# S5 windows loaded as one DMA a tile and masked on ScalarE, and z's three mixtures formed inside the LoRA products

## What is computed

```python
proj = n1 @ w_in                               # u | r | k | v | z, 512 columns each
# S5 group, on u: 32 groups of 16 channels, 64 complex states per group
x_t = a * x_(t-1) + bbar @ u_t                 # a scan over the tokens
y = c_re @ x_re - c_im @ x_im + d * u
z = gelu(y); out = z * sigmoid(z @ glu_w + glu_b)
# RWKV-7 group, on p = [r|k|v|z]
delta = shifted - p                            # the row before, minus this row
r = r_p + r_d * mu[0]; k = k_p + k_d * mu[1]; v = v_p + v_d * mu[2]
zw = z_p + z_d * mu[3]; za = z_p + z_d * mu[4]; zg = z_p + z_d * mu[5]
decay = exp(-DECAY_SCALE * sigmoid(w0 + tanh(zw @ w1) @ w2))
a = sigmoid(a0 + (za @ a1) @ a2)
g = sigmoid(zg @ g1) @ g2
```

## Time and profile before

| | us |
|---|---|
| median of 3 runs | 1459.41 (1457.45 to 1460.13) |
| the profiled execution | 1459.49 |
| its span | 1457.7 |
| TensorE busy | 1369.6 |
| VectorE busy | 444.9 |
| ScalarE busy | 253.7 |
| GpSimd busy | 55.4 |

### The profile page before, as it was taken

How to read it: one execution, slowest core, us unless ns; L and a number is a source line. 1 busy time by engine, 2 the same in 40 slices (tenths; PEclk the granted TensorE clock), 3 DMA queues, 4 the chain that set the end, 5 groups by cost and what they waited for, 6 DMA issues and landing times.

```text
span 1457.7 us, 21163 instructions
## 1 busy us (share of the span) xinstructions
PE 1369.6 (94%) x8649; PEld 695.7 (48%) x8649; DVE 444.9 (31%) x881; ACT 253.7 (17%) x480; POOL 55.4 (4%) x111
## 2 busy tenths in 40 slices
PE   8958999999999999999999999998998999988997
PEld 5735688866665633434334343343343433433442
DVE  5699846434121321312112111121121111311112
ACT  3223431212223212101101011011010110110102
POOL 4233000000000000000000000000000000000000
PEclk9978999999999999999999999999999999999999
DMA  8960121013939769999999999999999999999994
GB/s 325 203 116 30 62 91 60 32 60 120 388 135 410 279 252 397 401 423 428 427 428 428 428 428 428 428 428 428 428 428 428 428 428 428 428 429 425 428 426 179
DMA packets 43335, 471.84 MB, mean 324 GB/s; under 512 B 4992, under 2 KB 10368, under 8 KB 11520
## 3 DMA queue, kind: packets, MB, share of 16 engines
q1 hardware_dynamic: 37264, 461.42, 76.4%
q10 hardware_dynamic: 6000, 9.41, 3.3%
HBM read 465.33 MB, written 5.48 MB: 323 GB/s over the span
## 4 chain that ended last, share of the span: by engine, by line
PE 71%; DMA 20%; DVE 7%; issue 1%; ACT 1%; ACTq 0%; SPq 0%; DVEq 0%
DMA big<-in_w_gu 18%; PE bank L1189 16%; PE bank L1238 14%; PE bank L716 10%; PE bank L1112 5%; PE bank L979 2%; PE bank L799 2%; PE bank L1302 2%; PE bank L1258 2%; DMA big<-u_windows 2%; PE bank L898 1%; PE bank L1119 1%; PE bank L1214 1%; PE bank L1287 1%; DVE big L1847 1%
## 5 line engine op out<-in xcount | busy, mean ns | idle before, releaser
L1189 PE MATMUL bank<-big 128*64 128x512 f32 x1920 | 427.9, 603 | 27.6 <-DMA big<-in_w_gu 27.4
L1189 PEld LDWEIGHTS bank<-big 128*64 128x64 f32 x1920 | 147.1, 138 | 305.3 <-issue 295.0
L1238 PE MATMUL bank<-big 128*64 128x512 f32 x960 | 209.4, 594 | 0.0
L716 PE MATMUL bank<-big 128*128 128x320 f32 (+1 forms) x688 | 187.5, 430 | 9.1 <-DVE big L1922 6.8
L716 PEld LDWEIGHTS bank<-big 128*128 128x128 f32 x688 | 130.1, 191 | 63.0 <-issue 13.4
L2242 DVE TENSOR_TENSOR big<-big,bank 128x320 f32<-128x320 f32 x120 | 58.6, 488 | 303.0 <-PE bank L1258 297.8
L2228 DVE TENSOR_SCALAR big<-bank 128x512 f32<-128x512 f32 x32 | 22.2, 693 | 391.5 <-PE bank L1189 361.3
L1238 PEld LDWEIGHTS bank<-big 128*64 128x64 f32 x960 | 70.2, 137 | 127.9 <-issue 126.0
L1593 ACT ACTIVATE big<-big 128x512 f32<-128x512 f32 x30 | 18.8, 626 | 448.4 <-DVE big L2228 448.4
L1353 ACT ACTIVATE big<-bank 128x320 f32<-128x320 f32 (+3 forms) x122 | 53.1, 436 | 232.7 <-PE bank L716 41.9
L1112 PE MATMUL bank<-big 128*128 128x512 f32 x192 | 87.1, 603 | 1.4 <-DVE big L2176 1.4
(11 more groups left out here) (408 smaller groups left out, 1146.5 us busy)
## 6 DMA issues: line engine op xcount, KB each, us to landing
big<-in_w_gu SPq DMA_DIRECT2D x128, 2048.0 KB, 25.1
big<-in_w_down SPq DMA_DIRECT2D x62, 2048.0 KB, 22.3
big<-in_dense SPq DMA_DIRECT2D x47, 1024.0 KB, 8.4
big<-u_windows ACTq DMA_DIRECT2D x32, 160.0 KB, 10.4
big<-in_w_down SPq DMA_DIRECT2D x4, 1024.0 KB, 20.8
big<-in_smw SPq DMA_DIRECT2D x1, 1408.0 KB, 19.3
big<-in_xT SPq DMA_DIRECT2D x2, 640.0 KB, 4.6
big<-in_consts SPq DMA_DIRECT2D x1, 1028.5 KB, 14.5
```

What stands on the lines that cost most here:

```text
L716: last = mm(b[:, 0:n], w[:, k, :], src[:, k, :], start=(k == 0), stop=(k == kt - 1))
L1189: last = mm(ps[n][part, :], xte[:, 2 * j + k, part], w[s][:, k, n * 512:n * 512 + 512], start=False, stop=end)
L1238: last = mm(ps[bank][part, :], actT[:, 4 * d + i, part], w[s][:, i, h * 512:h * 512 + 512], start=(d == 0 and i == 0), stop=end)
```

## The change

- `u_windows` gets rows of 320 without zeros between them, channel by channel, the eight groups of a channel behind one another. Each tile of uT is stored by a DMA of its own (`store_rows`), as soon as its rows are there; seven zeros stand ahead of the first. The second u tile is scaled ahead of n1.
- A tile of windows is one DMA of 128 pieces of 10,240 B. What stands in the first columns of a row is then the end of the row before, which the mask takes away. Load 0 is issued between the memory squares and the last two stores, load 1 behind `memsum`, loads 2 and 3 from the list.
- All four masks are ScalarE's, seven activations each, and stand earlier in the list: `win` 0 ahead of k1, `win` 1 ahead of `c` 0.
- z's three mixtures are gone. (z + delta * mu) @ w is formed as z @ w + delta @ (mu * w): `delta` of z is kept in `z_apart`, ScalarE scales the twelve tiles of w1, a1 and g1 by mu (`weigh`), and `lora_up` has twenty-four matmuls.
- The order of the list is new from its third entry on.

```diff
--- before.py
+++ after.py
-MIX_ORDER = [("in", "k0"), ("memsum", 0), ("load", 0), ("in", "k1"), ("f", 0), ("in", "k2"), ("load", 1), ("c", 0), ("in", "k3"),
-             ("par", 0), ("memtotal", 0), ("in", "z0"), ("f", 1), ("in", "z1"), ("win", 0), ("win", 1), ("blk", 0), ("memroot", 0), ("load", 2), ("scan", 0),
-             ("y", 0), ("in", "z2"), ("mix", "k"), ("par", 1), ("in", "z3"), ("out", 0), ("c", 1), ("blk", 1), ("load", 3),
-             ("gelu", 0), ("scan", 1), ("gated", 0), ("y", 1), ("in", "r0"), ("win", 2), ("delta", "z"), ("in", "r1"), ("shares", 0),
-             ("shares", 1), ("out", 1), ("par", 2), ("c", 2), ("in", "r2"), ("blk", 2), ("scan", 2), ("y", 2), ("win", 3), ("gelu", 1), ("gated", 1),
-             ("shares", 2), ("in", "r3"), ("in", "v0"), ("mix", "r"), ("out", 2), ("par", 3), ("in", "v1"), ("c", 3), ("gelu", 2), ("gated", 2),
-             ("blk", 3), ("scan", 3), ("y", 3), ("lora_up", 0), ("in", "v2"), ("in", "v3"), ("kk", 0), ("memnorm", 0), ("out", 3),
-             ("gelu", 3), ("mix", "v"), ("gated", 3), ("lora_down", 0), ("knorm", 0), ("decays", 0), ("memk", 0), ("decay_exp", 0),
-             ("memk", 1), ("memk", 2), ("memk", 3), ("memk", 4), ("memk", 5), ("glu", 0)]
+MIX_ORDER = [("in", "k0"), ("memsum", 0), ("win", 0), ("in", "k1"), ("f", 0), ("in", "k2"), ("win", 1), ("c", 0), ("in", "k3"),
+             ("par", 0), ("memtotal", 0), ("in", "z0"), ("f", 1), ("blk", 0), ("load", 2), ("memroot", 0), ("par", 1), ("scan", 0), ("y", 0),
+             ("in", "z1"), ("mix", "k"), ("blk", 1), ("load", 3), ("out", 0), ("scan", 1), ("y", 1), ("win", 2), ("in", "z2"), ("c", 1),
+             ("win", 3), ("in", "z3"), ("out", 1), ("weigh", 0), ("par", 2), ("gelu", 0), ("gated", 0), ("c", 2), ("in", "r0"), ("delta", "z"),
+             ("blk", 2), ("scan", 2), ("y", 2), ("gelu", 1), ("in", "r1"), ("gated", 1), ("out", 2), ("par", 3), ("in", "r2"),
+             ("gelu", 2), ("c", 3), ("gated", 2), ("blk", 3), ("scan", 3), ("y", 3), ("in", "r3"), ("in", "v0"),
+             ("out", 3), ("mix", "r"), ("lora_up", 0), ("in", "v1"), ("memnorm", 0), ("in", "v2"), ("in", "v3"), ("kk", 0), ("gelu", 3),
+             ("mix", "v"), ("gated", 3), ("lora_down", 0), ("knorm", 0), ("decays", 0), ("memk", 0), ("decay_exp", 0), ("memk", 1),
+             ("memk", 2), ("memk", 3), ("memk", 4), ("memk", 5), ("glu", 0)]
...
-        u_dram = nc.dram_tensor("u_windows", [W5, T + 7], F32)
+        u_dram = nc.dram_tensor("u_windows", [W5 + 1, T], F32)
...
         def S(name):
...
+        z_apart, mu_w1, mu_a1, mu_g1 = R[4], view(RW[5], CT, 64), view(RW[5] + 256, CT, 64), view(RW[5] + 512, CT, P)
...
             def s5_block(ct):
...
-                if ct < 2:
-                    pe.wait_ge(S("uwin"), ct + 1)
-                else:
-                    pe.wait_ge(S("uwin_places"), (BL - 1) * (ct - 1))
+                pe.wait_ge(S("uwin"), (BL - 1) * (ct + 1))
...
             def lora_up():
...
-                pe.wait_ge(S("z_mixed"), 12)
-                for job, w, n, src in (("lw", smw("w1", CT, 64), 64, R[4]), ("la", smw("a1", CT, 64), 64, R[5]),
-                                       ("lg", smw("g1", CT, P), P, R[6])):
+                pe.wait_ge(S("z_apart"), 1)
+                pe.wait_ge(S("weighed"), 3 * CT)
+                for job, w, by, n in (("lw", smw("w1", CT, 64), mu_w1, 64), ("la", smw("a1", CT, 64), mu_a1, 64), ("lg", smw("g1", CT, P), mu_g1, P)):
...
-                        last = mm(b[0:n, 0:T], w[:, k, :], src[:, k, :], start=(k == 0), stop=(k == CT - 1))
+                        mm(b[0:n, 0:T], w[:, k, :], prj["z"][:, k, :], start=(k == 0), stop=False)
+                        last = mm(b[0:n, 0:T], by[:, k, :], z_apart[:, k, :], start=False, stop=(k == CT - 1))
...
             def lora_down():
...
+            def store_rows(ct):
+
+                stored(act, f"u{ct}")
+                to = bass.AP(u_dram, T + ct * P * T, [[T, 8], [8 * T, GC], [1, T]])
+                act.dma_start(to, uT[:, ct, 7:]).then_inc(S(f"u_stored{ct}"), 16)
+
+            def load_windows(ct):
+
+                if ct >= 2:
+                    computed(act, f"loc{ct - 2}")
+                act.wait_ge(S(f"u_stored{ct}"), 16)
+                act.wait_ge(S(f"u_stored{ct - 1}" if ct else "front_stored"), 16)
+                src = bass.AP(u_dram, T + ct * P * T - 7, [[1, BL], [8 * T, GC], [1, 8 * T]])
+                act.dma_start(uwins[ct % 2].rearrange("p g t -> p (g t)"), src).then_inc(S(f"uwin_in{ct % 2}"), 16)
+
+            act.wait_ge(S("u_pad"), 1)
+            act.dma_start(bass.AP(u_dram, T - 7, [[7, 1], [1, 7]]), uT[0:1, 0, 0:7]).then_inc(S("front_stored"), 16)
+            store_rows(0)
+            store_rows(1)
...
-            stored(act, "u3")
-            act.wait_ge(S("u_pad"), 1)
-            act.dma_start(u_dram.ap().rearrange("(c p) t -> p c t", p=P), uT).then_inc(S("u_stored"), 16)
+            load_windows(0)
+            store_rows(2)
+            store_rows(3)
...
             def s5_params(ct):
...
-            def load_windows(ct):
-
-                if ct >= 2:
-                    computed(act, f"loc{ct - 2}")
-                for tap in range(BL):
-                    src = bass.AP(u_dram, ct * P * (T + 7) + tap, [[T + 7, GC], [GC * (T + 7), 8], [1, T]])
-                    act.dma_start(uwins[ct % 2][tap * GC:(tap + 1) * GC], src).then_inc(S(f"uwin_in{ct % 2}"), 16)
-
             def mask_windows(ct):
...
-                act.wait_ge(S(f"uwin_in{ct % 2}"), 16 * BL * (ct // 2 + 1))
+                act.wait_ge(S(f"uwin_in{ct % 2}"), 16 * (ct // 2 + 1))
...
-                    step(af(w[:, j::BL], w[:, j::BL], ACT.Identity, scale=con("window")[:, j:j + 1]), "uwin_places")
-
-            act.wait_ge(S("u_stored"), 16)
+                    step(af(w[:, j::BL], w[:, j::BL], ACT.Identity, scale=con("window")[:, j:j + 1]), "uwin")
+
...
             for kind, n in MIX_ORDER:
...
                 elif kind == "load":
...
-                elif kind == "win" and n >= 2:
+                elif kind == "win":
...
                 elif kind == "memsum":
...
+                    load_windows(1)
                 elif kind == "memroot":
...
+                elif kind == "weigh":
+                    act.wait_ge(S("smw_in"), 16)
+                    for m, (w, by) in enumerate(((smw("w1", CT, 64), mu_w1), (smw("a1", CT, 64), mu_a1), (smw("g1", CT, P), mu_g1))):
+                        for k in range(CT):
+                            step(af(by[:, k, :], w[:, k, :], ACT.Identity, scale=vec("rwkv_mu", 4 * (3 + m) + k)), "weighed")
                 elif kind == "blk":
...
+            u_rows(1)
...
-            u_rows(1)
...
-            def delta(c):
+            def delta(c, d):
...
-                ps_, ds_ = (x[:, :, TP:T].rearrange("p i (s t) -> p i s t", s=NB) for x in (p, DELTA))
-                step(tt(DELTA[:, :, 1:TP], p[:, :, 0:TP - 1], p[:, :, 1:TP], sub))
-                step(ts(DELTA[:, :, 0:1], p[:, :, 0:1], -1.0, None, mul))
+                ps_, ds_ = (x[:, :, TP:T].rearrange("p i (s t) -> p i s t", s=NB) for x in (p, d))
+                step(tt(d[:, :, 1:TP], p[:, :, 0:TP - 1], p[:, :, 1:TP], sub))
+                step(ts(d[:, :, 0:1], p[:, :, 0:1], -1.0, None, mul))
...
-                step(tt(ds_[:, :, :, 0], prev[:, n], ps_[:, :, :, 0], sub))
-
-            def share(c, dst, mu):
+                step(tt(ds_[:, :, :, 0], prev[:, n], ps_[:, :, :, 0], sub), "z_apart" if c == "z" else None)
+
+            def mixes(c):
+                p = prj[c]
+                delta(c, DELTA)
...
-                    last = stt(dst[:, i, :], DELTA[:, i, :], vec("rwkv_mu", 4 * mu + i), prj[c][:, i, :], mul, add)
-                    step(last, "z_mixed" if c == "z" else ("delta_free" if (c, i) == ("v", 3) else None))
-
-            def mixes(c):
-                delta(c)
-                share(c, prj[c], "rkv".index(c))
+                    last = stt(p[:, i, :], DELTA[:, i, :], vec("rwkv_mu", 4 * "rkv".index(c) + i), p[:, i, :], mul, add)
+                    step(last, "delta_free" if (c, i) == ("v", 3) else None)
...
             def f_matrices(ct):
...
-            def mask_windows(ct):
-
-                dve.wait_ge(S(f"uwin_in{ct % 2}"), 16 * BL * (ct // 2 + 1))
-                step(tt(uwins[ct % 2], uwins[ct % 2], over(con("window"), 1, 8), mul), "uwin")
-
             def s5_local(ct):
...
                 elif kind == "delta":
-                    delta(n)
-                elif kind == "shares":
-                    share("z", R[4 + n], 3 + n)
+                    delta(n, z_apart)
                 elif kind == "memnorm":
...
                 elif kind == "f":
...
-                elif kind == "win" and n < 2:
-                    mask_windows(n)
                 elif kind == "c":
...
                 elif kind == "y":

```

## The result

The changed kernel takes 1489.38 us (median of 4 runs, 1483.92 to 1492.09) against 1459.77 (1457.45 to 1463.21) for the kernel before: a ratio of 1.0196, 95% interval 1.0161 to 1.0231. It is 2% slower, where 0.3% faster was forecast. The profiled execution is the slowest of the four, 1492.09 us with a span of 1490.3.

A forecast was written before the change was run, and what follows sets the result against it. TensorE's path to `memk`, held up by VectorE's chain, was taken as the bound: 110.7 + 58.8 = 169.5 us against 173.9, −4.4, so 1459.5 − 4.4 = 1455.1 us. Range 1447 to 1460.5 us.

The forecast's parts named there:

- 128 pieces over 16 engines 3.2 us: Window loads: a tile's 10 KB pieces spread over 16 engines; with 1.7 us to land, a tile in after 5 us.
- The upper bound of 12 us: Window loads: slowest landing assumed, 10 us at the small pieces' time per byte plus 1.7; block 0 then 4.5 us late.
- the line: Window loads: packet time against size, from 1.14 KB at 139 ns and 8.2 KB at 336 ns; 10 KB takes some 395.
- The row of 139 ns: Old window loads, 88 to 100 us: 1152 packets averaging 1.14 KB, 139 ns each, held 16 engines for 83.4%.
- C: Rival, chance 0.10: ScalarE's masks hold everything up; load 0 landing at 52 gives 1469 us, over 0.2% slower from 46.
- the walk: Mixer's step-by-step timeline on VectorE and TensorE, `blk` 0 at 54.3, `memk` at 169.5; 1451.5 to 1457 us, chance 0.56.
- B: Rival, chance 0.17: window pieces are no faster; loads of 12 us, `blk` 0 4.5 us late, 1459.6 us, no change.
- A: Rival, chance 0.17: VectorE's chain shorter than walked, through lighter GpSimd F or a timely tanh; 1444 to 1451 us.
- the parts listed for the 4.4 us: Gain at `memk`: gaps cost 17.2 + 3.7 instead of 24.2 + 5.7, small waits gain 1.6, the loss is 6.7.
- VectorE's chain: Mixer: scan 0 at 56.7 instead of 75.85, c 1 ends 83.9, tanh wait 5.4 us, scan 2 ends 109.2.
- The gap before `out` 2: TensorE in the mixer, after r1: idle from 101.1 to 110.7, 9.6 us, waiting on scan 2, then cold.
- The restart: TensorE after the idle before `out` 2: `out` 2 with `par` 3 cold at 5.8 us, then r2 at 4.4.

The follow-up runs named there:

- e9: Changed kernel with window partitions numbered 8 channel + tap, so each tile's one load has the 16 channels outermost: 1463.06 us, ratio to before 1.0016.
- e11: e9 with each tile's load cut into two DMAs of 8 channels, so 8 is outermost: 1488.68 us.
- e4: Changed kernel with eight DMAs a tile, one a tap, each 16 pieces of 10,240 B with channels outermost: 1475.86 us.
- e7: Changed kernel with two DMAs a tile, four taps and 64 pieces of 10,240 B each: 1510.71 us.
- e2: Changed kernel with the taps of a window load's source written as 4 x 2, still one DMA a tile: 1488.19 us.
- e5: e4 with every tap read from the same aligned place in DRAM, S5 output not the reference's: 1473.14 us.
- e8: Kernel before with only the mask of tile 1 moved behind y 0, loads as before: 1455.63 us, ratio 0.9965.

## Why the prediction was wrong

**The step that failed** is in the part on the window loads: "128 pieces over 16 engines 3.2 us". The row gave a time per packet; that 16 engines would share them was taken for granted, though the source's outermost dimension stands in the diff. The upper bound of 12 us assumed the 16 too, and so held none of the four landings. e9 and e11 put this step at 25.6 of the 29.6 us; the forecast missed by 34.3 (1489.4 against 1455.1).

**The piece's own time** was the second term that was too small: 0.395 us by the line, 0.76 in the changed kernel (50.9% of 9 us x 16, over 96) and 0.69 in e9, where a load landed after 8.7 to 14.4 us and not after 5. The line took a weight's piece for a window's. The fastest piece of the changed kernel did take 0.38 us.

**Piece size.** The row of 139 ns, completions counted in, was read as small pieces going slowly, and new ones going fast for their size. The new ones did go faster, 13.4 B/ns against 8.4, but size is not the reason: e4's pieces are of the new size and went at 8.8, and ScalarE's stores into `u_windows`, of 1,280 B as well, took 55 ns in the median of the changed kernel. The Trainium skill's rule, 512 B and up at line rate (DMA: Bandwidth & Descriptors, the opening table), was set aside for a row that could not speak against it. By that rule, going from 1,280 to 10,240 B gains nothing, and 8.4 beside 8.8 B/ns agree. Why a window's piece is slower than a weight's, 24.4 B/ns by the earlier trace rows, stays open.

**The rivals.** What happened is C in its outcome, ScalarE's masks holding everything up, given 0.10, through a cause named in no rival. Load 0 landed at 46.8, past C's threshold of 46. C's own slope, 14 us for a landing at 52, gives 8.8 for that; it became 20.4, since load 1, queued behind load 0 on the same 8 engines, came at 66.7. From block 0 to `memk` the changed kernel takes 128.7 us (74.75 to 203.49), the walk 115.2: loads 2 and 3 hold the masks again, and the tanh waits 17.6 us behind mask 3, the scaled weights and `par` 2. B was wrong in cause and size: the new pieces went faster for each byte, and still landed later than its 12 us. A did not occur. In the sum, the parts listed for the 4.4 us (24.2 + 5.7 - 17.2 - 3.7 + 1.6 - 6.7) make 3.9.

**VectorE's chain** held where e9 lets it be seen. From scan 0 to the end of c 1 it took 27.6 us (59.57 to 87.20), in the walk 27.2; the wait for the tanh was 6.4 us, in the walk 5.4; `out` 2 came at 113.65, in the walk 110.7, 2.9 of it because F is written in steps of eight numbers in e9 (scan 0 at 59.57 instead of 56.7). Of the six operations of F 1 four took 1.07 to 1.10 us instead of 0.69; the first of them, the last, and the scan:

```profile
53.63 1.08 DVE L1877 TENSOR_TENSOR big<-big 128x512 f32<-128x512 f32 x1
...
58.44 1.10 DVE L1882 TENSOR_TENSOR big<-big 128x512 f32<-128x512 f32 x1
59.57 0.59 DVE L1910 TENSOR_TENSOR big<-big 128x256 f32<-128x256 f32 x1
```

**Gaps and clock.** The gap before `out` 2 was 10.8 us (walk 9.6). The one before `out` 1 was 2.1 instead of 7.6, as TensorE itself came later; it cost nothing more, since VectorE set its end. The restart was mis-sized: from `out` 2 to the end of r2 5.8 + 4.4 = 10.2 us were assumed, and it took 15.4 (113.65 to about 129.1). The windows of e9:

```profile
113.60:122.40 8.80, 7.63 (x153) 7.41 (x153) 6.07 (x11) 2.11 (x4) 0.00 (x0) 0.50 0.01 4
122.40:129.10 6.70, 6.70 (x19) 4.21 (x21) 2.61 (x4) 0.46 (x2) 0.00 (x0) 0.67 0.00 0
...
126.00:127.00 1.00, 1.00 (x3) 0.58 (x3) 0.00 (x0) 0.00 (x0) 0.00 (x0) 0.62 0.00 0
127.00:128.00 1.00, 1.00 (x5) 0.71 (x4) 0.00 (x0) 0.00 (x0) 0.00 (x0) 1.00 0.00 0
```

and of the kernel before, after its second gap:

```profile
109.00:110.00 1.00, 1.00 (x7) 1.00 (x6) 0.93 (x3) 0.60 (x1) 0.00 (x0) 0.53 0.00 0
110.00:111.00 1.00, 1.00 (x12) 1.00 (x11) 0.93 (x3) 0.60 (x1) 0.00 (x0) 1.00 0.00 0
```

The clock is at the lower level when `out` 2 starts, and rises at about 126.8, after 13.1 us, across a halt of 1.1 inside `out` 2. In the kernel before it rose at about 109.9, 4.2 us after `out` 1 started, with no halt. (The 2.2 us of the earlier trace rows are the length of that window.) With the restart, 7.4 us are explained: `memk` at 176.88 in e9 against 169.5 is F's 2.9 and the restart's 5.2, less 0.7 for all the rest. So the forecast gain of 4.4 would not have been there with good loads either.

**z.** `lora_up` took 13.2 us (168.38 to 181.53), forecast 13.4. The scaled weights took 4.74 us, within 2.4 to 5.3, but with the cover gone: they stand in the path behind mask 3.

## What to carry to other kernels

Before a DMA is reshaped, read the outermost dimension of both sides and compare the queue's share of 16 engines in a stretch where it runs alone: the pieces' time says nothing about how many carry them. A time per piece holds for the stream it was read from; before a slow row is put down to the size of its pieces, look for pieces of that size that go elsewhere. And work moved into the queue of an engine that also frees banks makes each late transfer late for everything behind it.

## What the runs showed of the hardware

- A DMA of ScalarE's queue ran on 8 engines with 8 outermost (50.9% in the changed kernel, 53.3% in e11), on 4 with 4 (26.5%), and two such DMAs on the same 4 (e7). Taps written as 4 x 2 ran no slower than as 8 (e2: 45.8% from 80 to 89 us).
- A completion, a packet of 4 B, took an engine 16 ns (e9) to 29 ns (before). A piece of 10,240 B took 0.69 us in e9, 0.76 in the changed kernel, 1.16 in e4.
- Reading 4 bytes off a boundary cost 3.7% (e4, e5).
- TensorE halts in the midst of a job without a releaser: 7.47 us two records into the `in` behind `out` 0 in the changed kernel, 7.04 there in e11, 2.13 in e9, 1.1 to 1.7 inside `out` 2, and with the old loads 3.00 in block 1 of e8 and 0.23 in the kernel before. In the 14 traces there are 21 such halts from 40 to 180 us, and each ends 1.3 to 1.9 us after a packet of 16,384 B of the queue named `q8 instruction`. In the changed kernel it is this one, from 95 to 97 us:

```profile
q8 instruction: 1, 0.02, 3.2%
```

It runs from 95.45 to 96.47, and TensorE goes on at 98.03. Load 2 had landed at 95.42; in e11 the packet starts at 95.14 and load 2 landed at 94.90. That TensorE waits for its own instructions, and they for the window load on their DMA engine, fits all of this; no run was made to test it.
